# Fifteen of a layer's 22 up-projection block pairs from seven block products in place of eight, in a four-layer streaming encoder step

## The reference

```python
def rmsnorm(x, g):
    y = xf * lax.rsqrt(jnp.mean(xf * xf, axis=-1, keepdims=True) + EPS)
    return (y * g.astype(jnp.float32)).astype(x.dtype)

def swiglu_ffn(x, w_in, w_out):          # w_in (1024, 5632), w_out (2816, 1024)
    g, u = jnp.split(x @ w_in, 2, axis=-1)
    return (jax.nn.silu(g) * u) @ w_out
```

## Time and profile before

| | |
|---|---|
| median of 3 runs | 2667.25 us |
| span of the profiled execution | 2663.1 us |
| around it (launch and end, median less span) | 4.15 us |
| TensorE matmul busy | 2645.5 us, 99% |
| VectorE busy | 1266.0 us, 48% |
| ScalarE busy | 964.1 us, 36% |
| GpSimd busy | 171.9 us, 6% |
| DMA | 229.69 MB, mean 86 GB/s |
| granted TensorE clock | 0.999 of full, full in all 40 slices |

### The profile page before, as it was taken

One profiled execution on the slowest core, in us unless ns is written; L12 is line 12 of the kernel. 1 busy time (PEld: TensorE's weight loads), 2 busy tenths in 40 slices (PEclk: granted clock), 3 DMA queues, 4 the chain that ended last, 5 costly groups with the idle time before them and its releaser, 6 DMA issues.

```text
span 2663.1 us, 50175 instructions
## 1 busy us (share of the span) xinstructions
PE 2645.5 (99%) x20893; PEld 2581.1 (97%) x20893; DVE 1266.0 (48%) x1732; ACT 964.1 (36%) x1454; POOL 171.9 (6%) x182
## 2 busy tenths in 40 slices
PE   8999999999999999999999999999999999999998
PEld 8999999999988999999998899999999999999998
DVE  5565442444555554334457554433445554442442
ACT  5554221223555532222245643222234543221233
POOL 2101000001000100000112210000011101000001
PEclk9999999999999999999999999999999999999999
DMA  3223233232433223323322222232332222232232
GB/s 114 76 66 91 84 96 86 84 91 78 124 98 104 77 83 92 93 79 90 90 67 79 72 83 79 87 95 79 91 84 84 69 80 82 87 98 77 86 99 78
DMA packets 440460, 229.69 MB, mean 86 GB/s; under 512 B 15780, under 2 KB 436864, under 8 KB 440336
## 3 DMA queue, kind: packets, MB, share of 16 engines
q1 hardware_dynamic: 438688, 226.89, 29.5%
q10 hardware_dynamic: 1200, 0.59, 0.1%
q0 software_dynamic: 448, 0.45, 0.1%
HBM read 219.03 MB, written 8.87 MB: 86 GB/s over the span
## 4 chain that ended last, share of the span: by engine, by line
PE 96%; DVE 2%; issue 1%; ACT 0%; DMA 0%; DVEq 0%; ACTq 0%
PE slot L1838 87%; PE aux L1806 2%; PE aux L2219 1%; PE aux L1983 1%; PE aux L2225 1%; PE aux L2131 1%; PE aux L2069 1%; PE aux L1998 1%; DVE w_lo L1164 0%; PE aux L2001 0%; PE aux L1948 0%; PE aux L1873 0%; PE aux L2008 0%; PE slot L2278 0%; DVE lru_i L1635 0%
## 5 line engine op out<-in xcount | busy, mean ns | idle before, releaser
L1838 PE MATMUL slot<-xg_hi,w_hi 128*128 128x272 f32 x4352 | 917.0, 292 | 4.1 <-DVE gla_sq L1182 2.3
L1838 PE MATMUL slot<-xg_hi,w_lo 128*128 128x272 f32 x4352 | 900.0, 288 | 0.0
L1838 PE MATMUL slot<-xg_lo,w_hi 128*128 128x272 f32 x4352 | 897.9, 288 | 0.0
L1838 PEld LDWEIGHTS slot<-xg_hi,w_hi 128*128 128x128 f32 x4352 | 682.9, 188 | 16.3 <-issue 9.3
L1838 PEld LDWEIGHTS slot<-xg_lo,w_hi 128*128 128x128 f32 x4352 | 683.5, 188 | 0.0
L1838 PEld LDWEIGHTS slot<-xg_hi,w_lo 128*128 128x128 f32 x4352 | 679.9, 189 | 0.0
L1164 DVE TENSOR_TENSOR w_lo<-raw,w_hi 128x1024 fp32r<-128x1024 f32 (+3 forms) x367 | 479.0, 1305 | 243.1 <-ACT w_hi L619 235.0
L619 ACT ACTIVATE w_hi<-raw 128x1024 fp32r<-128x1024 f32 (+4 forms) x369 | 409.2, 1109 | 337.1 <-PE slot L1838 325.7
L1838 PE MATMUL slot<-h_hi,w_hi 128*128 128x272 f32 x1386 | 286.1, 288 | 0.0
L1838 PE MATMUL slot<-h_hi,w_lo 128*128 128x272 f32 x1386 | 286.0, 287 | 0.0
L1838 PE MATMUL slot<-h_lo,w_hi 128*128 128x272 f32 x1386 | 285.7, 287 | 0.0
(11 more groups left out here) (317 smaller groups left out, 2348.7 us busy)
## 6 DMA issues: line engine op xcount, KB each, us to landing
raw<-in_l_ffn_w_in_dram SPq DMA_DIRECT2D x176, 512.0 KB, 3.8
raw<-in_l_ffn_w_out_dram SPq DMA_DIRECT2D x64, 704.0 KB, 4.6
raw<-in_l_gla_w_in_dram SPq DMA_DIRECT2D x48, 512.0 KB, 3.8
raw<-in_l_att_w_qkv_dram SPq DMA_DIRECT2D x24, 512.0 KB, 3.8
raw<-in_l_lru_w_in_dram SPq DMA_DIRECT2D x24, 512.0 KB, 3.9
raw<-in_l_gla_w_out_dram SPq DMA_DIRECT2D x16, 512.0 KB, 4.0
raw<-in_l_lru_w_out_dram SPq DMA_DIRECT2D x7, 768.0 KB, 4.7
att_bias<-bias_scratch SPq DMA_DIRECT2D x8, 512.0 KB, 4.0
```

The source lines that it names most:

```text
L1838: ins = pe.matmul(slot[par][:, hf, 0:HALF], w[par][:, k, :], a[:, k0 + k, hf * HALF:(hf + 1) * HALF], start=(k == 0 and at == 0), stop=(k ...
```

## The change

In 15 of a layer's 22 up pairs (kind "S" in `UP_PAIRS`; "C" stays as it was) the pair is taken as a 2 x 2 block problem: the two weight blocks g and u, each cut in two along the input features (4 tiles, `KQ`), against x cut in two along the features and the tokens. Seven products of sums replace the eight: 7 x 4 tiles x 3 = 84 matmuls of 272 columns in place of 96. The second half of the last layer stays as it was, so there are 7 such pairs in each of the four first halves and 8 in each of three second halves, 52 in all.

- Sums of x tiles are formed once a layer (`t_high`, `t_low`), in the first three pairs of `up0`: one, two and one of the four steps.
- Sums of weight tiles are formed for every S pair, in the window of the pair before it (`w_sums`, on VectorE), then split in high and low parts (`hi_sums`, `hi_a11`, `hi_more_sums`, `hi_rest` on ScalarE; `lo_sums`, `lo_a11`, `lo_more_sums`, `lo_rest` on VectorE).
- Inside the seven products the outputs are combined by ScalarE copies (`copy_product`) and VectorE additions (`c_plus_d`, `a_plus_b`, `c_d_added`, `last_quarter`, `scale_g`).
- The two weight blocks of an S pair are loaded by two DMAs one behind the other, into buffer A (the two old `raw` buffers as one) or B (a new one); within a run the pairs take A, B, A, B.
- The u block is no longer multiplied by 1/rms. The down-projection's result is, before it is added to `x`: one more VectorE instruction in each of 56 down blocks.
- The up loops of the seven changed halves are written out. Semaphores of the start are merged.

The core of the diff, where order and waits stand:

```diff
+KQ = XT // 2
+UP_PAIRS = ("CCCSSSSCSSS", "CSSSSCSSSSC")
+T_PART = {0: (0,), 1: (1, 2), 2: (3,)}
...
+                        to_b = s_buf[i, hf, u] == "B"
+                        sp.wait_ge(s_lo, b - 2 if to_b else b)
+                        into = w_raw((i, hf, u))
+                        sp.dma_start(into[:, 0:XT, :], wi[:, :, u_at:u_at + P]).then_inc(s_rawb if to_b else s_raw[b0 % 2], 16)
+                        sp.dma_start(into[:, XT:2 * XT, :], wi[:, :, g_at:g_at + P]).then_inc(s_rawb if to_b else s_raw[1 - b0 % 2], 16)
...
+            def hi_rest(at, b):
...
+                act.wait_ge(s_mm, b)
+                act.activation(tiles_apart(w_his, w_slots(b % 2)[5]), tiles_apart(w_raw(at), KQ), ACT.Copy).then_inc(s_hi, 2)
...
+            def t_high(i, q):
+                n, norm = KQ * i + q, f"l{i}_norm_ffn"
+                if n:
+                    act.wait_ge(s_tdve, 4 * n)
+                act.activation(FF["xq"][:, 0:2, :].rearrange("p a n -> p (a n)"), one(x, q), ACT.Copy, scale=gain(norm, q))
+                act.activation(FF["xq"][:, 2:4, :].rearrange("p a n -> p (a n)"), one(x, q + KQ), ACT.Copy,
+                               scale=gain(norm, q + KQ)).then_inc(s_tact, 1)
+                act.wait_ge(s_tdve, 4 * n + 3)
+                act.activation(one4(FF["t_hi"], q), FF["tq"][:, :, :], ACT.Copy).then_inc(s_tact, 1)
...
+            def up_window(i, hf, u, kinds):
...
+                if now == "S":
+                    if prev == "C":
+                        hi_a11(at, b, prev)
+                    hi_rest(at, b)
+                else:
+                    split(b + 1, 1 - p0, XT)
+                if hf == 0 and u == 0:
+                    stat(stat_of[i, "ffn"])
+                if prev == "S":
+                    silu(i, hf, u - 1, kinds)
+                if now == "S":
+                    copy_product(at, p0, "d")
+                if u:
+                    h_high(i, hf, u - 1, kinds)
+                if now == "S":
+                    copy_product(at, p0, "b")
+                if now == "S" and nxt == "S":
+                    hi_sums((i, hf, u + 1), b + 2, now)
+                for q in T_PART.get(u, ()) if hf == 0 else ():
+                    t_high(i, q)
+                if nxt == "S":
+                    if now == "S":
+                        hi_a11((i, hf, u + 1), b + 2, now)
+                    else:
+                        hi_sums((i, hf, u + 1), b + 2, now)
+                    hi_more_sums((i, hf, u + 1), b + 2, now)
+                else:
+                    split(b + 2, p0, XT if nxt else FH)
+                if now == "C":
+                    silu(i, hf, u, kinds)
...
-                        dve.tensor_tensor(halves(one(x, m)), slot[(p0 + j) % 2][:, :, 0:HALF], halves(one(x, m)),
-                                          ALU.add).then_inc(s_free, 1)
+                        if scaled:
+                            if j:
+                                dve.wait_ge(s_xd, m + split_tiles(i, name) - XT)
+                            dve.tensor_tensor(FF["y"][:, 2 * j:2 * j + 2, :], slot[(p0 + j) % 2][:, :, 0:HALF], halves(rstd[:, :]),
+                                              ALU.mult).then_inc(s_free, 1)
+                            dve.wait_ge(s_free, b + 1)
+                            dve.tensor_tensor(one(x, m), FF["gu"[j]], one(x, m), ALU.add).then_inc(s_xd, 1)
...
+            def w_sums(at, b):
+                r, s, n, to = w_raw(at), FF["s"], 3 * s_no[at], sum_at(b % 2)
+                raw_landed(at, b)
+                dve.tensor_tensor(tiles8(s, to[0]), tiles8(r, KQ), tiles4(r, 0).unsqueeze(1).broadcast_to([P, 2, KQ * P]),
+                                  ALU.add).then_inc(s_ws, 1)
+                dve.wait_ge(s_ws, n + 1)
+                dve.tensor_tensor(tiles4(s, to[2]), tiles4(s, to[0]), tiles4(r, 2 * KQ), ALU.add).then_inc(s_ws, 1)
+                dve.wait_ge(s_ws, n + 2)
+                dve.tensor_tensor(tiles4(s, to[3]), tiles4(s, to[2]), tiles4(r, 3 * KQ), ALU.add).then_inc(s_ws, 1)
...
+            def t_low(i, q):
+                n, xq, tq = KQ * i + q, FF["xq"], FF["tq"]
+                dve.wait_ge(s_tact, 2 * n + 1)
+                dve.tensor_tensor(tq[:, 0:2, :], xq[:, 0:4:3, :], xq[:, 1:2, :].broadcast_to([P, 2, HALF]),
+                                  ALU.subtract).then_inc(s_tdve, 1)
+                dve.wait_ge(s_tdve, 4 * n + 1)
+                dve.scalar_tensor_tensor(tq[:, 2, :], xq[:, 3, :], -1.0, tq[:, 0, :], ALU.mult, ALU.subtract).then_inc(s_tdve, 1)
+                dve.wait_ge(s_tdve, 4 * n + 2)
+                dve.scalar_tensor_tensor(tq[:, 3, :], tq[:, 2, :], -1.0, xq[:, 2, :], ALU.mult, ALU.subtract).then_inc(s_tdve, 1)
+                dve.wait_ge(s_tact, 2 * n + 2)
+                dve.tensor_tensor(one4(FF["t_lo"], q), tq[:, :, :], one4(FF["t_hi"], q).bitcast(F32),
+                                  ALU.subtract).then_inc(s_tdve, 1)
...
+            def up_window(i, hf, u, kinds):
...
+                if prev == "S":
+                    scale_g(before, b - 2, p0)
+                if prev == "C":
+                    product(i, hf, u - 1, kinds)
+                if now == "S":
+                    if prev == "C":
+                        lo_a11(at, b, 3)
+                    lo_rest(at, b)
+                else:
+                    split(b + 1, 1 - p0, XT)
+                if hf == 0 and u == 0:
+                    stat(stat_of[i, "ffn"], rstd)
+                if prev == "S":
+                    last_quarter(before)
+                if now == "S":
+                    if prev == "S":
+                        product(i, hf, u - 1, kinds)
+                    c_plus_d(at, p0)
+                    if nxt == "S":
+                        w_sums(after, b + 2)
+                    a_plus_b(at, p0)
+                    if nxt == "S":
+                        lo_sums(after, b + 2)
+                    h_low(i, hf, u - 1)
+                    if nxt == "S":
+                        lo_a11(after, b + 2, 2)
+                        lo_more_sums(after, b + 2, 3)
+                    else:
+                        split(b + 2, p0, XT if nxt else FH)
+                    c_d_added(at, p0)
+                    return
+                if prev == "S":
+                    product(i, hf, u - 1, kinds)
+                if u:
+                    h_low(i, hf, u - 1)
+                for q in T_PART.get(u, ()) if hf == 0 else ():
+                    t_low(i, q)
+                if nxt == "S":
+                    w_sums(after, b + 2)
+                dve.wait_ge(s_mm, b + 1)
+                dve.tensor_tensor(FF["y"][:, 0:2, :], up_banks(hf, u, p0)[0][:, :, 0:HALF], halves(rstd[:, :]),
+                                  ALU.mult).then_inc(s_free, 1)
+                if nxt == "S":
+                    lo_sums(after, b + 2)
+                    lo_more_sums(after, b + 2, 2)
+                else:
+                    split(b + 2, p0, XT if nxt else FH)
...
+            def seven_products(i, hf, u, b):
...
+                a11_second = up_kinds(i, hf, layers)[u - 1] == "S"
+                pe.wait_ge(s_free, b - 2)
+                pe.wait_ge(s_tdve, 4 * KQ * (i + 1))
+                pe.wait_ge(s_wl, 3 * n + 1)
+                times(c, at[0], *from_t(0), True, True)
+                times(d_, at[1], *from_t(1), True, True).then_inc(s_pr, 1)
+                pe.wait_ge(s_wl, 3 * n + (3 if a11_second else 2))
+                times(b_, at[2], *from_t(2), True, True).then_inc(s_mm, 1)
+                pe.wait_ge(s_wl, 3 * n + 3)
+                times(a, at[4], *from_x(0, 0), True, True).then_inc(s_pr, 1)
+                pe.wait_ge(s_out7, 5 * n + 1)
+                times(c, at[3], *from_x(KQ, 1), False, True).then_inc(s_pr, 1)
+                pe.wait_ge(s_lo, b + 2)
+                times(d_, at[5], *from_t(3), False, True).then_inc(s_pr, 1)
+                pe.wait_ge(s_out7, 5 * n + 2)
+                times(a, at[6], *from_x(KQ, 0), False, True).then_inc(s_mm, 1)
```

More of the change, by code:

```diff
@@ L152, in schedule, with up_kinds, up_plan @@
     return base, at
+def up_kinds(i, hf, layers):
+    return None if (i, hf) == (layers - 1, 1) else UP_PAIRS[hf]
+def up_plan(layers):
+    number, buffer, n = {}, {}, 0
+    for i in range(layers):
+        for hf in range(2):
+            run = 0
+            for u, kind in enumerate(up_kinds(i, hf, layers) or ""):
+                run = run + 1 if kind == "S" else 0
+                if run:
+                    number[i, hf, u], buffer[i, hf, u] = n, "AB"[(run - 1) % 2]
+                    n += 1
+    return number, buffer, n
 def encoder_step(nc, d, o, layers=4):
     base, total_blocks = schedule(layers)
+    s_no, s_buf, n_seven = up_plan(layers)
+    b_no = {at: n for n, at in enumerate(at for at in s_no if s_buf[at] == "B")}
     stat_of, n_stat = {}, 0
@@ L300, in encoder_step @@
         s_sg, s_h, s_hhi, s_hlo = sem("ffn_silu"), sem("ffn_h"), sem("h_hi"), sem("h_lo")
```

(37 more changed lines are left out.)

334 lines of the change are left out of this document (258 added, 76 removed).

## The result

The changed kernel takes 2675.44 us (median of 6 runs, 2675.23 to 2682.54) against 2667.16 us for the kernel before (6 runs, 2664.78 to 2668.97): a ratio of 1.0035, with a 95% interval of 1.0024 to 1.0047. It is slower by 0.3%, 8.3 us between the medians, where 13 us less were forecast. In all six executions the time is 1.7 us longer than the span. So the profiled execution of before took some 2664.8 us, the fastest of its six, and 2.5 of the 4.15 us that the forecast put around the span were the spread between executions. The two profiled executions lie 17.7 us apart, of which 9 are such a spread and 8 the change.

A forecast was written before the change was run, and what follows sets the result against it. TensorE was taken to bound the kernel: -78.2 + 31.5 + 7.5 + 7.2 + 18.5 + 0.3 = -13.2 us, so a span of 2649.9 and a time of 2654 us. The 8-in-10 range was 2615 to 2675.

The forecast's parts named there:

- The bound: Whole kernel: TensorE, busy for 99% of the span, sets the time at 0.1253 us a matmul.
- the gain: S pairs: 12 fewer matmuls save 1.504 us in each of 52 pairs, 78.2 us; a pair then takes 10.53 us.
- The late load: Second window of each run: third pair's load comes late, `a_plus_b` stalls TensorE 2.25 us, 14 times, 31.5 us.
- Starts of runs: Window before a run: late load delays TensorE 0.66 us in second runs, 0.97 in first runs of `up1`; 7.5 us.
- First down block: Behind the short run of `up0`: the block's load is issued late, 1.8 us four times, 7.2 us.
- Sums of x at the second and third pair: Start of `up0`: sums of x delay low parts by 2.5 and 2.1 us in each of four layers, 18.5 us.
- Rest of the change: 1/rms behind the down-projection costs 0.3 us, once, before the second gated linear attention; written-out loops cost nothing.
- The clock: Whole kernel: TensorE's granted clock stays full behind stalls of 2 us, so no time was added.
- (b): Rival: third pair's data is there when `w_sums` asks, so the loads don't matter; 2615 us, chance 0.20.
- (c): Rival: VectorE becomes the bound in S windows, its work 10.4 of 10.53 us; up to 2691 us, slower, chance 0.20.
- The rule weighed against the change: VectorE in S windows: each of fifteen instructions would cost its full length, 0.08 us above start-to-start distance, giving 2691 us.

The follow-up runs named there:

- the run with short waits: Fourteen waits of TensorE for one piece of zeros from VectorE, put into the changed kernel with eight products everywhere (2667.01 us): 2687.50 us.
- the kernel with long waits: Fourteen waits of TensorE for two pieces of zeros from VectorE, put into the changed kernel with eight products everywhere (2667.01 us): 2715.33 us.
- the long runs: Rows of eight and nine S pairs, 59 in all, against the 2595.38 us kernel with early loads and moved sums of x: 2586.14 us.

## Why the prediction was wrong

**The bound, the gain.** Right. S windows without a wait take 10.53 us for 84 matmuls at 0.1253, and with the waits gone and the same 52 pairs 72 of the 78.2 us are in the time (2595.4).

**The late load.** Right in place and size: 35.5 us in 14 waits, said 31.5. The load landed 5.8 us after its issue, the forecast had 5.4, and a few waits are up to 3.7 us long.

**The small terms.** These were off. Starts of runs: 12.9 us in 12 waits for `lo_sums`, said 7.5. First down block: 1.5 and 1.6 us in two of four places, said four times 1.8. Sums of x at the second and third pair: 2.1 us four times and 4.6 in all (18.5 said, 13.1 measured). The errors cancel, and the sum of 64.8 us is as good as it is by luck. Rest of the change: 0, said 0.3. In the bounds a landing of 5.9 gives 2666 by the prediction's own 2.4 us for each 0.1, not 2668.

**What a wait costs beside its idle time.** Missed. The forecast took the shift of TensorE's start from the walk, and the rows give the idle time; the run with short waits has 0.21 us between the two. 37 new waits x 0.21 = 7.8 us, if the others cost what those fourteen did.

**The clock.** This is the step that failed. The prediction put it as "The granted clock is full in all slices of the page, also where TensorE waits 1.9 us at a time, so I take no change of the clock for stalls of 2 us." Thirteen waits of 1.9 to 3.7 us were followed by half the clock in the profiled execution, some 20 us. The sum had this term at nothing. The trace of before had too few waits to say anything: one of some 2.3 us at 28 us, with the full clock behind it, as this row of the kernel before shows in the same columns:

```profile
28.16:32.16 4.00, 4.00 (x32) 1.00 0.91 252
```

The same wait of 2.3 us in the changed kernel has the half clock:

```profile
28.29:32.29 4.00, 4.00 (x22) 0.64 0.91 248
```

In the kernel with long waits it is one in two. So a single wait without a loss was read as a rule, and the page's clock line, with slices far wider than such a stretch, could not have shown one either. The sum with it: 2663.1 - 78.2 + 64.8 + 7.8 + 20 = 2677.5 against a span of 2680.8. 3 us are unassigned.

The Trainium skill, "TensorE: Matmul & The Clock Gate", HAM oscillation — how this bites in real kernels, tells of a kernel whose waits between groups of matmuls bring the clock down again and again, and puts the cost at half of the time at the low clock. The runs here agree: 1.6 us for a stretch of 3.4. A rival by that rule, with the 22 waits of 2 us and more that the walk gave, was missing among my cases. By the measured price and one in two it would have been 11 x 1.6 = 18 us on the forecast, 2672 us.

**The rivals.** (b) gave the late load no weight, and issuing it a window earlier is worth 51 us. (c) had the right sign for the wrong reason: VectorE keeps pace at 98%. The rule weighed against the change ("VectorE: DVE Perf Modes" of the Trainium skill, The DRAIN you can't avoid: the next instruction doesn't start before the pipe is empty) was taken without the last sentence of the same paragraph, by which an instruction that isn't held starts earlier. The S windows agree with that sentence: the third sum of 512 elements (L2013) is 0.69 long and the next instruction starts 0.61 behind its start, and in the long runs VectorE's fifteen instructions, 11.27 us by their lengths, fit into 10.53.

## What to carry to other kernels

Where TensorE runs without a break, don't price a new wait at its idle time. Here a wait of 1.25 us cost 1.46, and one of 2.3 us cost 3.45 on the mean, since TensorE ran at half its clock for 3.4 us behind every second one; all sixteen waits of 3 us and more in these profiles had it. And when a change gives the bound engine less work, walk each queue through the shorter window with the waits as written: a load that was allowed one window too late took back most of the gain, and one condition on SP returned 51 us. The walk found this load before anything ran; what it lacked was the price of the waits. A step that is a chain of hand-overs fills its queue for its whole length, not for its busy time.

## What the runs showed of the hardware

Not expected by the forecast: of 14 equal waits of 2.32 us in one execution 7 are followed by half the clock and 7 are not. All 14 of 1.25 us had the full clock. The half clock lasted some 3.4 us (granted clock 0.57 over 4 us), matmuls of 272 columns then start 0.227 us apart in place of 0.1253. VectorE held 15 instructions with waits between them, some over two pieces or with a broadcast, in 10.53 us at 98% busy. What decides which of the equal waits is followed by the half clock is open.
